# Sum into x, second norm and the next stage's first eight units in halves of 320 tokens, in a two-layer transformer trunk

## The chip, the cores and the metric

The kernel runs on one core of a Trainium2 chip. TensorE multiplies matrices, VectorE (DVE in the profile), ScalarE (ACT) and GpSimd (POOL) do elementwise work, SyncE (SP) issues most transfers; all follow their own instruction streams and meet at semaphores. The metric is the device time of one launch in microseconds (us). A change under about half a per cent can't be told from none.

## The reference

A trunk of two layers over two token streams, 512 sampled tokens and 128 prompt tokens, with model width 1024, all in float32. Each layer is:

```python
def trunk_layer(x, mod, g_mix_pre, g_mix_post, g_ffn_pre, g_ffn_post, w_ffn_in, w_ffn_conv, w_ffn_out, mixer):
    shift1, scale1, gate1, shift2, scale2, gate2 = mod
    h = rmsnorm(x, g_mix_pre) * (1 + scale1) + shift1
    y, ctx_state = mixer(h)
    x = x + gate1 * rmsnorm(y, g_mix_post)
    h = rmsnorm(x, g_ffn_pre) * (1 + scale2) + shift2
    x = x + gate2 * rmsnorm(conv_ffn(h, w_ffn_in, w_ffn_conv, w_ffn_out), g_ffn_post)
    return x, ctx_state
```

`rmsnorm` divides a token by the root of the mean of its squares over the 1024 features. `mixer` is a projection (12 blocks of 128 outputs in layer 0, 18 in layer 1), attention of several kinds and an output projection. `conv_ffn` projects to 2 x 2816, convolves each feature along the tokens with three taps, multiplies silu(gate) by value, and projects back. `mod` are six vectors per stream and layer, made from a conditioning vector by a wide projection.

## The kernel before

Everything is feature-major: a tensor is `[128 partitions, 8 blocks, 640 tokens]`, with the 512 sampled tokens ahead of the 128 prompt tokens. `x`, `y`, and the two parts `hh` and `hl` of the stage's input lie in SBUF.

A **unit** is one block of 128 outputs over all 640 tokens. A float32 product is made from three products of shorter numbers: weights `raw` (512 KB, loaded by SyncE) are split by ScalarE into a high part `whi` (`hi`, L499) and by VectorE into the rest `wlo` (`lo`, L793); the input is split the same way. `unit` (L1373, L1374) makes eight blocks x three products x two halves of 320 tokens, 48 matmuls; the first half's result goes to `bankA[s]`, the second's to `bankB[s]`, with s the parity of the unit. `raw`, `whi`, `wlo` and the banks all have two slots: the split for unit u+2 is made when unit u has been multiplied (`s_unit`), and SyncE loads weights n when the low part n-2 is made (`wide`, `s_lo`). The phases and their unit numbers stand in `UNITS`, and every wait counts in them.

Behind each unit the engines take its result out: in a feed-forward input phase (`fin0`, `fin1`, 22 units each, in pairs of gate and value) ScalarE copies the first half (L527), VectorE the second (L845), ScalarE makes the middle tap (L725), VectorE the two outer ones (L1143, L1146), and each pair ends with silu, gate product and a split into `ffh` and `ffl`. In layer 0 VectorE also sums a "modulation chunk" a pair (L801, two passes), a piece of the projection that makes `mod`, from a ring that SyncE loads (`chunk_in`), and SyncE waits for `s_mused` before it loads the next. In layer 1's input phase (`in`) VectorE applies the rotary embedding to four blocks (`rope`, L972 to L978) instead.

**The boundaries.** Three times a stage that makes `y` is followed by a sum into x, a second norm and a dense stage: post norm 1 then pre norm 2 (layer 0), post norm 3 then the pre norm 4 (into layer 1), post norm 5 then pre norm 6 (layer 1). There, before the change:

- `post_norm`: `deviation` (square root of the token sums, ScalarE), `reciprocal` (VectorE, L861), `spread` (TensorE copies the 640 inverse values to all partitions, L1438); then for each of the eight blocks VectorE multiplies y by the inverse rows (L867), adds gate times that to x (L899, once for each stream), ScalarE squares the new x (L534) and TensorE sums the squares over the features (`stat`, L1428).
- `pre_norm`: deviation, reciprocal and spread again; then for each block VectorE multiplies x by the inverse (L867), ScalarE scales and shifts (L557, once for each stream), and copies to `hh` (L563), and VectorE makes `hl` (L887).
- `first_pair` (L1486, L1487): the first two units of the next stage side by side, block by block as `hl` comes. All further units follow in order (`dense_pairs`).

## Time and profile before

| | us |
|---|---|
| median of 3 runs | 1804.48 |
| lowest, highest | 1798.44, 1805.21 |
| the profiled execution, its own time | 1804.35 |
| its span | 1802.6 |
| TensorE busy | 1659.5 (92%) |
| VectorE busy | 1092.2 (61%) |
| ScalarE busy | 722.5 (40%) |
| GpSimd busy | 114.5 (6%) |
| mean granted TensorE clock | 0.961 |

The span runs from the first to the last instruction of the profiled execution, and 1.8 us lie around it. Matmuls overlap, so a TensorE matmul's duration (0.31) is longer than the distance to the next one. Instructions of VectorE and ScalarE overlap the next by some 0.08.

### The profile page before, as it was taken

The page shows a single profiled execution, that of the slowest core. Times are in us where ns is not written, and L with a number is a line of the kernel's source. Part 1 is how long each engine was busy: PE and PEld are TensorE (multiplying, and loading weights), DVE is VectorE, ACT ScalarE, POOL GpSimd, SP SyncE. Part 2 cuts the span into 40 slices and gives each one's busy share as a digit, 9 for nine tenths or more (in the row PEclk, how much of TensorE's full clock was granted, in tenths as well). Part 3 has the DMA queues.
Part 4 walks back from the last instruction along what each step waited for, and adds up shares of the span by engine and source line. Part 5 has one row for each costly group of instructions (what it writes and reads, how often), then busy time and mean ns, then how long its engine had stood idle before and what let it go on. Part 6 is the DMA issues. An engine that isn't in the chain of part 4 may idle for free.

```text
span 1802.6 us, 33042 instructions
## 1 busy us (share of the span) xinstructions
PE 1659.5 (92%) x12288; PEld 1586.0 (88%) x12288; DVE 1092.2 (61%) x2046; ACT 722.5 (40%) x1186; POOL 114.5 (6%) x121
## 2 busy tenths in 40 slices
PE   5799899969999999999889979989799999999995
PEld 1799687959999999999889968779699999999995
DVE  4497676767777767777753248762566651466524
ACT  3722665226343134442241138652366541343410
POOL 1060210000000000000000032500000000000000
PEclk7899899979999999999999979999899999999998
DMA  8233001422434533345322110102012222222211
GB/s 295 89 110 124 31 2 48 157 77 72 118 113 142 199 116 114 105 145 193 120 79 81 48 62 2 45 1 62 32 59 71 80 81 72 70 71 80 92 49 59
DMA packets 42768, 160.63 MB, mean 89 GB/s; under 512 B 5072, under 2 KB 6096, under 8 KB 42304
## 3 DMA queue, kind: packets, MB, share of 16 engines
q1 hardware_dynamic: 39888, 152.00, 25.7%
q0 software_dynamic: 1584, 6.61, 1.1%
q8 instruction: 54, 0.88, 0.2%
q10 hardware_dynamic: 1216, 0.92, 0.2%
q14 instruction: 26, 0.21, 0.0%
HBM read 155.98 MB, written 3.54 MB: 88 GB/s over the span
## 4 chain that ended last, share of the span: by engine, by line
PE 79%; DVE 6%; issue 4%; ACT 2%; DMA 1%; DVEq 1%; ACTq 0%; SPq 0%
PE ps L1373 28%; PE ps L1374 28%; PE ps L1537 4%; PE ps L1566 4%; PE ps L1412 3%; PE ps L1552 3%; PE ps L1428 2%; PE ps L1486 1%; DMA ring<-in_wmodt 1%; DVE x L899 1%; PE ps L1487 1%; PE ps L1387 1%; PE ps L1386 1%; DVE ring L801 1%; DVE wlo L793 1%
## 5 line engine op out<-in xcount | busy, mean ns | idle before, releaser
L499 ACT ACTIVATE whi<-raw 128x1024 fp32r<-128x1024 f32 (+1 forms) x166 | 185.6, 1120 | 603.5 <-PE ps L1374 505.1
L1373 PE MATMUL ps<-hh,whi 128*128 128x320 f32 x920 | 286.7, 312 | 12.9 <-DVE wlo L793 12.9
L1373 PE MATMUL ps<-hl,whi 128*128 128x320 f32 x920 | 285.1, 310 | 0.0
L1373 PE MATMUL ps<-hh,wlo 128*128 128x320 f32 x920 | 285.1, 310 | 0.0
L1374 PE MATMUL ps<-hl,whi 128*128 128x320 f32 x920 | 285.0, 310 | 0.0
L1374 PE MATMUL ps<-hh,whi 128*128 128x320 f32 x920 | 284.9, 310 | 0.0
L1374 PE MATMUL ps<-hh,wlo 128*128 128x320 f32 x920 | 284.9, 310 | 0.0
L793 DVE TENSOR_TENSOR wlo<-raw,whi 128x1024 fp32r<-128x1024 f32 (+1 forms) x166 | 219.5, 1324 | 75.2 <-ACT whi L499 74.8
L1373 PEld LDWEIGHTS ps<-hh,whi 128*128 128x128 f32 x920 | 173.1, 188 | 14.5 <-DVE wlo L793 14.5
L1374 PEld LDWEIGHTS ps<-hh,whi 128*128 128x128 f32 x920 | 173.2, 188 | 0.0
L1374 PEld LDWEIGHTS ps<-hl,whi 128*128 128x128 f32 x920 | 173.2, 188 | 0.0
L1374 PEld LDWEIGHTS ps<-hh,wlo 128*128 128x128 f32 x920 | 173.2, 188 | 0.0
L1373 PEld LDWEIGHTS ps<-hh,wlo 128*128 128x128 f32 x920 | 173.1, 188 | 0.0
L1373 PEld LDWEIGHTS ps<-hl,whi 128*128 128x128 f32 x920 | 173.1, 188 | 0.0
L1428 PE MATMUL ps<-onesd,work 128*128 128x128 f32 x640 | 91.3, 301 | 31.3 <-ACT work L534 31.3
L1428 PEld LDWEIGHTS ps<-onesd,work 128*128 128x128 f32 x640 | 85.5, 212 | 36.1 <-ACT work L534 20.3
L653 ACT ACTIVATE pb<-pb,stat 128x640 f32<-128x640 f32 (+3 forms) x140 | 97.2, 697 | 11.6 <-DVE stat L1038 11.3
L1373 PE MATMUL ps<-ffh,whi 128*128 128x320 f32 x308 | 96.3, 313 | 0.0
L725 ACT ACTIVATE work<-work,wconv 128x642 f32<-128x642 f32 x88 | 73.5, 835 | 55.3 <-DVE work L845 36.1
L1373 PE MATMUL ps<-ffh,wlo 128*128 128x320 f32 x308 | 95.3, 310 | 0.0
L1373 PE MATMUL ps<-ffl,whi 128*128 128x320 f32 x308 | 95.3, 309 | 0.0
L1374 PE MATMUL ps<-ffh,wlo 128*128 128x320 f32 x308 | 95.3, 309 | 0.0
(209 smaller groups left out, 3322.1 us busy)
## 6 DMA issues: line engine op xcount, KB each, us to landing
raw<-in_w SPq DMA_DIRECT2D x134, 512.0 KB, 3.6
work<-in_wmodt SPq DMA_DIRECT2D x54, 512.0 KB, 3.6
raw<-in_w SPq DMA_DIRECT2D x32, 704.0 KB, 4.2
ring<-in_wmodt SPq DMA_DIRECT2D x26, 512.0 KB, 3.7
work<-in_wmod SPq DMA_DIRECT2D x16, 512.0 KB, 5.0
work<-in_rpb POOLq DMA_DIRECT2D x8, 480.0 KB, 4.3
x<-in_x SPq DMA_DIRECT2D x1, 2560.0 KB, 17.4
out_x<-x SPq DMA_DIRECT2D x8, 320.0 KB, 2.2
```

The lines of the kernel that those rows point to most:

```text
L499: nc.scalar.activation(whi[:, s, 0:kk * P], raw[:, s, 0:kk * P], ACT.Copy).then_inc(s_hi, 1)
L653: nc.scalar.activation(probs, probs, ACT.Exp, bias=negm, scale=-1.0, accum_out=sums[:, job.unit, half:half + 1]).then_inc(s_p, 1)
L725: nc.scalar.activation(cb[s], ub[s][:, 1:1 + CW], ACT.Copy, scale=wconv[:, bass.ds(2 * h + (2 * f0 + s), 1), 1]).then_inc(s_c1, 1)
L793: V.tensor_tensor(wlo[:, s, 0:kk * P], raw[:, s, 0:kk * P], whi[:, s, 0:kk * P].bitcast(F32), ALU.subtract).then_inc(s_lo, 1)
L801: last = V.scalar_tensor_tensor(out=out, in0=ring[b], scalar=1.0, in1=cwide[:, st, :], op0=ALU.mult, op1=ALU.mult, accum_out=mod[:, st, ba ...
L1373: T.matmul(bankA[s], slot(w, s, k), h[:, k, 0:HT], start=st, stop=sp_)
L1374: last = T.matmul(bankB[s], slot(w, s, k), h[:, k, HT:NT], start=st, stop=sp_)
L1412: last = T.matmul(out, h[:, k, t * P:(t + 1) * P], w[:, :, k * P:(k + 1) * P], start=k == 0 and n == 0, stop=k == KD - 1 and n == 2)
L1428: ins = T.matmul(token_sums[:, t, :], sq[s][:, t * P:(t + 1) * P], onesd[:, :], start=first and t in (0, 4), stop=last and t in (3, 4))
L1537: ins = T.matmul(scores_of(job, c, c + w), q[job.rows, job.pair, job.q0:job.q0 + P], k[job.rows, job.kslot, k0:k0 + w], start=n == 0, stop ...
L1552: T.transpose(turned_probs[half][:, c:c + P], pb[j % 4][:, c:c + P], ident[:, :])
L1566: T.matmul(values_bank[job.rows, 0:P], v[:, t, job.v_col:job.v_col + DH], pts[:, job.half, c:c + P], start=i == 0, stop=i == len(keys) - 1)
```

## The change

At the three boundaries the tokens are treated in halves of 320. The first half (tokens 0 to 319) is all sampled tokens; the second has 192 sampled and 128 prompt tokens. A class `Half` holds each half's token range and its semaphores. The next stage's first eight units are made twice: first all eight for the first half (`half_unit` on `bankA`, 24 matmuls each), then all eight for the second (`bankB`). As only two units' weights fit, SyncE loads these eight a second time and ScalarE and VectorE split them a second time, so every unit number behind a boundary rises by eight (`OFF`, `evicted`). The first half's results are parked in `y` (or `qk` for layer 1's input) as they come. The convolution, the gate and the rotary embedding need both halves and follow the second pass, where ScalarE takes the first half from `y` and not from the bank. Sums of squares, deviation, reciprocal and spread exist once for each half. The order on each engine is written out by hand in three functions called `norm_boundary`. In layer 0 SyncE's queue around the first modulation chunks is written anew. The work of the two norms on each element is the same.

The diff, cut to its core:

```diff
-            for n in (22, 23, 24):
+            for n in range(22, 28):
                 wide(n, n % 2, w8, n, 8)
-            sp.wait_ge(s_t, 24)
+            sp.wait_ge(s_mused, 26)
             chunk_in(26, 1, ring1)
-            wide(25, 1, w8, 25, 8)
+            for j in range(4):
+                wide(28 + j, j % 2, w8, 20 + j, 8)
             sp.wait_ge(s_mused, 27)
             chunk_in(27, 1, ring1)
+            for j in range(4, 6):
+                wide(28 + j, j % 2, w8, 20 + j, 8)
...
+            def half_squares(m, half, k0, k1):
+                for k in range(k0, k1):
+                    act.wait_ge(half.stat, half.squares(m) + k + 1)
+                    act.wait_ge(half.tu, half.items(m - 1) + k + 3)
+                    act.nop(nofuse=True)
+                    nc.scalar.activation(sq[k % 2][:, half.f:half.t], x[:, k, half.f:half.t],
+                                         ACT.Square).then_inc(half.sq, 1)
...
+            def half_high(m, half, layer, which, k0, k1):
+                part_ = 0 if which == 0 else 3
+                for k in range(k0, k1):
+                    s = k % 2
+                    act.wait_ge(half.t_, half.items(m) + k + 1)
+                    act.wait_ge(half.hl, half.made(m) + k + 1)
+                    for st, f, e in half.segments:
+                        last = nc.scalar.activation(hf[s][:, f:e], tn[s][:, f:e], ACT.Identity,
+                                                    scale=coef[:, layer, st, which, k:k + 1],
+                                                    bias=mod_col(layer, part_, st)[:, k:k + 1])
+                    last.then_inc(half.tu, 1)
+                    act.wait_ge(half.tu, half.items(m) + k + 3)
+                    nc.scalar.activation(hh[:, k, half.f:half.t], hf[s][:, half.f:half.t],
+                                         ACT.Copy).then_inc(half.hh, 1)
...
+            def norm_boundary(n, phase, ready, evac):
...
+                def split_and_take(j):
+                    act.wait_ge(s_unit, ua + j + 3)
+                    hi(j % 2, KD, (ua + j) // 2 + 1)
+                    evac(j, j % 2)
...
+                deviation(n)
+                half_squares(m, FIRST, 0, 8)
+                half_deviation(m, FIRST)
+                act.wait_ge(s_coef, ready)
+                half_high(m, FIRST, layer, which, 0, 8)
+                half_squares(m, SECOND, 0, 2)
+                split_and_take(0)
+                split_and_take(1)
+                half_squares(m, SECOND, 2, 4)
+                split_and_take(2)
+                split_and_take(3)
+                half_squares(m, SECOND, 4, 8)
+                split_and_take(4)
+                half_deviation(m, SECOND)
+                split_and_take(5)
+                half_high(m, SECOND, layer, which, 0, 3)
+                split_and_take(6)
+                half_high(m, SECOND, layer, which, 3, 6)
+                split_and_take(7)
+                half_high(m, SECOND, layer, which, 6, 8)
...
-                    copy_a(ub[s][:, 1:1 + HT], s)
-                    act.wait_ge(s_fa, u + 3)
-                    act.wait_ge(s_fb, u + 3)
+                    if parked:
+                        nc.scalar.activation(ub[s][:, 1:1 + HT], part(y, 2 * h + s, 0, HT), ACT.Copy).then_inc(s_park, 1)
+                        act.wait_ge(s_park, 2 * h + (8 * layer + s + 1))
+                    else:
+                        copy_a(ub[s][:, 1:1 + HT], s)
+                        act.wait_ge(s_fa, u + (3 - OFF[phase]))
+                    act.wait_ge(s_fb, u + (3 - OFF[phase]))
...
+            def norm_boundary(n, phase):
...
+                def split_for(j):
+                    dve.wait_ge(s_unit, ua + j + 3)
+                    lo(j % 2, KD, ua + j + 2)
+
+                reciprocal(n)
+                dve.wait_ge(s_row, n + 1)
+                post_items(FIRST, 0, 8)
+                post_items(SECOND, 0, 4)
+                half_reciprocal(m, FIRST)
+                dve.wait_ge(s_row, m + 1)
+                pre_row(FIRST, 0)
+                pre_row(FIRST, 1)
+                for k in range(KD):
+                    half_low(m, FIRST, k)
+                    pre_row(FIRST, k + 2)
+                post_items(SECOND, 4, 6)
+                split_for(0)
+                split_for(1)
+                post_items(SECOND, 6, 8)
+                split_for(2)
+                split_for(3)
+                split_for(4)
+                half_reciprocal(m, SECOND)
+                split_for(5)
+                dve.wait_ge(SECOND.row, SECOND.index(m) + 1)
+                pre_row(SECOND, 0)
+                pre_row(SECOND, 1)
+                for k in range(KD):
+                    if k == 2:
+                        split_for(6)
+                    if k == 5:
+                        split_for(7)
+                    half_low(m, SECOND, k)
+                    pre_row(SECOND, k + 2)
...
+            def half_unit(half, u, off, chunks=None):
+                bank, free = ((bankA, s_fa), (bankB, s_fb))[half.second]
+                cols = slice(half.f, half.t)
+                both = (u, u + 1) if chunks is not None else (u,)
+                pe.wait_ge(s_lo, both[-1] + 1)
+                pe.wait_ge(free, both[-1] + 1 - off)
                 for k in range(KD):
+                    if chunks is not None:
+                        pe.wait_ge(half.hl, chunks + k + 3)
+                    for v in both:
+                        for n, (w, h) in enumerate(((whi, hh), (whi, hl), (wlo, hh))):
+                            ins = T.matmul(bank[v % 2], slot(w, v % 2, k), h[:, k, cols], start=k == 0 and n == 0,
+                                           stop=k == KD - 1 and n == 2)
+                        if k == KD - 1:
+                            ins.then_inc(s_unit, 1)
...
+            def norm_boundary(n, phase):
+                m = n + 1
+                ub_ = UNITS[phase][0]
+                ua = ub_ - 8
+                for k in range(KD):
+                    half_stat(m, FIRST, k)
+                half_spread(m, FIRST)
+                half_unit(FIRST, ua, evicted[0], FIRST.made(m))
+                half_unit(FIRST, ua + 2, evicted[0])
+                for k in range(2):
+                    half_stat(m, SECOND, k)
+                half_unit(FIRST, ua + 3, evicted[0])
+                for k in range(2, 5):
+                    half_stat(m, SECOND, k)
+                half_unit(FIRST, ua + 4, evicted[0])
+                for k in range(5, 8):
+                    half_stat(m, SECOND, k)
+                half_unit(FIRST, ua + 5, evicted[0])
+                half_spread(m, SECOND)
+                half_unit(FIRST, ua + 6, evicted[0])
+                half_unit(FIRST, ua + 7, evicted[0])
+                evicted[0] = OFF[phase]
+                half_unit(SECOND, ub_, evicted[0], SECOND.made(m))
+                for j in range(2, 8):
+                    half_unit(SECOND, ub_ + j, evicted[0])
...
-                        first_pair(u0, 8 * (2 * layer + 1))
-                        dense_pairs(u0 + 2, FH - 1)
+                        norm_boundary(norm_index(layer, 1), (layer, "fin0"))
+                        dense_pairs(u0 + 8, FH - 4)
```

## Rows read from the trace of the kernel before

**Rows 1.** The page: busy time, and the chain that ended last

```profile
PE 1659.5 (92%) x12288; PEld 1586.0 (88%) x12288; DVE 1092.2 (61%) x2046; ACT 722.5 (40%) x1186; POOL 114.5 (6%) x121
...
PE 79%; DVE 6%; issue 4%; ACT 2%; DMA 1%; DVEq 1%; ACTq 0%; SPq 0%
```

**Rows 2.** Timeline of ScalarE, layer 0's feed-forward input: start, duration, instruction

```profile
453.62 1.06 ACT L499 ACTIVATE whi<-raw 128x1024 fp32r<-128x1024 f32 x1 [2.77 <-PE ps L1374]
...
467.70 1.06 ACT L499 ACTIVATE whi<-raw 128x1024 fp32r<-128x1024 f32 x1 [2.77 <-PE ps L1374]
```

**Rows 3.** Timeline of VectorE at the three boundaries, first rows and a reciprocal

```profile
382.89 1.55 DVE L867 TENSOR_TENSOR work<-y,ps 128x640 f32<-128x640 f32 x2 [2.60 <-PE ps L1438]
...
887.83 1.55 DVE L867 TENSOR_TENSOR work<-y,ps 128x640 f32<-128x640 f32 x2 [1.47 <-PE ps L1438]
...
1279.57 1.55 DVE L867 TENSOR_TENSOR work<-y,ps 128x640 f32<-128x640 f32 x2 [1.47 <-PE ps L1438]
...
1297.27 0.19 DVE L861 RECIPROCAL std<-std 128x5 f32<-128x5 f32 x1 [2.85 <-ACT std L540]
```

**Rows 4.** Timeline of TensorE at the third boundary

```profile
1303.22 0.61 PE L1486 MATMUL ps<-hh,whi 128*128 128x320 f32 x1 [4.32 <-DVE hl L887]
...
1303.63 0.47 PE L1487 MATMUL ps<-hh,whi 128*128 128x320 f32 x1
...
1303.89 0.47 PE L1486 MATMUL ps<-hl,whi 128*128 128x320 f32 x1
...
1322.42 0.41 PE L1373 MATMUL ps<-hh,whi 128*128 128x320 f32 x1 [2.98 <-DVE wlo L793]
```

**Rows 5.** Timeline of VectorE and SyncE behind the first boundary

```profile
423.80 1.23 DVE L793 TENSOR_TENSOR wlo<-raw,whi 128x1024 fp32r<-128x1024 f32 x1
...
436.12 0.33 SPq L396 DMA_DIRECT2D work<-in_wmodt  x1
...
436.48 1.21 DVE L793 TENSOR_TENSOR wlo<-raw,whi 128x1024 fp32r<-128x1024 f32 x1
```

**Rows 6.** Timeline of VectorE behind the second boundary

```profile
928.18 1.22 DVE L793 TENSOR_TENSOR wlo<-raw,whi 128x1024 fp32r<-128x1024 f32 x1 [0.65 <-ACT whi L499]
...
935.43 0.69 DVE L978 TENSOR_TENSOR qk<-y 128x512 f32<-128x512 f32 x1
```

**Rows 7.** Groups by shape: count | busy us, mean ns | idle before

```profile
L867 DVE TENSOR_TENSOR work<-y,ps 128x640 f32<-128x640 f32 x32 | 25.9, 821 | 10.9 <-PE ps L1438 7.0 <-DVE x L899 3.9
...
L899 DVE SCALAR_TENSOR_TENSOR x<-work,coef,x 128x512 f32 x24 | 17.9, 746 | 0.0
...
L899 DVE SCALAR_TENSOR_TENSOR x<-work,coef,x 128x128 f32 x24 | 8.3, 346 | 0.0
...
L845 DVE COPY y<-ps 128x320 f32 x26 | 12.7, 488 | 87.8 <-PE ps L1374 68.8 <-PE ps L1487 16.6 <-PE ps L1387 2.4
...
L557 ACT ACTIVATE work<-work,mod,coef 128x512 f32<-128x512 f32 x32 | 25.9, 810 | 11.2 <-DVE work L867 11.1
...
L557 ACT ACTIVATE work<-work,mod,coef 128x128 f32<-128x128 f32 x32 | 15.3, 480 | 0.0
...
L527 ACT ACTIVATE work<-ps 128x320 f32<-128x320 f32 x90 | 37.8, 420 | 0.0
```

**Rows 8.** The chain that ended last, one block of sums of squares

```profile
1257.54 1.11 PE ps L1428 x10
```

**Rows 9.** Timeline of VectorE behind the third boundary

```profile
1321.14 1.22 DVE L793 TENSOR_TENSOR wlo<-raw,whi 128x1024 fp32r<-128x1024 f32 x1 [1.90 <-ACT whi L499]
...
1332.89 1.23 DVE L793 TENSOR_TENSOR wlo<-raw,whi 128x1024 fp32r<-128x1024 f32 x1 [0.95 <-ACT whi L499]
```

**Rows 10.** The page, transfers: KB each, us from issue to landing

```profile
raw<-in_w SPq DMA_DIRECT2D x134, 512.0 KB, 3.6
```

**Rows 11.** Windows: stretch, us, busy by engine, granted TensorE clock, DMA

```profile
1302.90:1308.40 5.50, 5.18 (x22) 5.21 (x23) 4.11 (x7) 5.07 (x9) 0.00 (x0) 0.59 0.00 0
...
1322.40:1328.00 5.60, 5.58 (x38) 5.58 (x39) 4.64 (x7) 4.08 (x6) 0.00 (x0) 1.00 0.39 102
```

More of the change, by code:

```diff
@@ L1171, in ffn @@
             def ffn(layer):
[L1172 removed]
+                dve.wait_ge(SECOND.hl, SECOND.made(4 * layer + 2) + 8 + 2)
                 for s in range(2):
@@ new lines, in half_spread @@
+            def half_spread(m, half):
+                pe.wait_ge(half.rec, half.index(m) + 1)
+                if half.second:
+                    pe.wait_ge(s_t, FIRST.items(m))
+                    pe.wait_ge(half.t_, half.items(m))
+                c0 = 8 if half.second else 0
+                rows = half_rows[half.second]
+                for i, (c, r) in enumerate(((0, 0), (P, 0), (2 * P, 64))):
+                    w = P - r
+                    ins = T.matmul(rows[:, c:c + w], std[:, c0 + i:c0 + i + 1].to_broadcast([P, P]), ident[:, r:P],
+                                   start=True, stop=True)
+                ins.then_inc(half.row, 1)
```

203 lines of the change are left out of this document (142 added, 61 removed).

## The prediction

> **What bounds the kernel now.** I read the page's first part and its chain of waits first: TensorE is busy 92% of the span, and 79% of the chain that ended last is TensorE's [rows 1]. So wherever the dense units run, the time is TensorE's. One unit (48 matmuls of 320 columns) takes 7.04 us: in the stretch at 454 us the split of every second unit starts 14.08 us after the last, twice 7.04 [rows 2]. Time can be won only where TensorE stands still, and time is lost wherever it is made to.
>
> The change touches three boundaries, which I call A (layer 0, attention output to feed-forward), B (layer 0 to layer 1) and C (layer 1, attention output to feed-forward). I count each from the first post-norm row on VectorE (time 0) to the first matmul of the ninth unit behind it. The timelines show for C: time 0 at 1279.57, the second norm's reciprocal 17.7 later, the first dense matmul 23.65 later, the third unit 42.85 later [rows 3, 4]. Six more units make 42.2, so the ninth unit starts at 85.1. In A and B the low split that releases the third unit starts 40.9 and 40.35 in [rows 3, 5, 6] and takes 1.23, so the third unit starts at 42.2 and 41.6, the ninth at 84.4 and 83.8. Eight units are 56.3 of each, so a boundary now costs some 28 us of idle TensorE. That is all that could be won: three times 28.
>
> **Durations used.** On VectorE 640 columns take 0.82 and 320 take 0.49; the next instruction starts 0.08 before that ends, so a row of 320 costs 0.41. The add to x is 0.75 for 512 columns and 0.35 for 128: about 0.55 for 320 in one piece, 0.42 and 0.35 for the second half's two pieces (192 and 128). On ScalarE a 320-column copy or square takes 0.42; the scale-and-shift 0.81 for 512 and 0.48 for 128, so 0.65 for 320 and 0.53 and 0.48 for two pieces [rows 7]. A weight split is 1.06 on ScalarE [rows 2] and then 1.23 on VectorE [rows 5]. A full block of sums of squares is ten matmuls in 1.11 [rows 8], so the half block's six are 0.68. A hand-over between engines or to an engine's own result is taken as 0.12 to 0.2. With these the old order gives 23.7 and 43.3 for C where the trace has 23.65 and 42.85, so I trust them to about half a microsecond.
>
> **The new order, step by step.**
> *First half to its first matmul.* Eight rows and adds of 320 columns pace at 0.41 + 0.47 + 0.2 = 1.08 and end at 8.4. Then VectorE does four items of the second half (1.2 each) before it looks at the deviation, which is ready at 10.5: the reciprocal goes at 12.8. Spread, row, scale, copy and low part (0.7, 0.49, 0.65, 0.42, 0.49 and five hand-overs) bring the first matmul at 16.7. Against 23.65 that wins 7.0.
> *First half's pair.* ScalarE's scale and copy pace each chunk at 1.2 where its six matmuls take 0.88, so the pair ends at 26.2; the split of the third unit's weights (1.06 + 1.23, begun when the first unit of the pair ends at 25.8) lets the third half-unit start at 28.4. Before, 42.85 stood here, but with 14.1 us of matmuls done against 7.0 now.
> *Six first-half units.* 6 x 3.52 = 21.1, and the second half's eight sum blocks and its spread now stand between them on TensorE: 9 x 0.68 = 6.1. Square 4 of the second half waits on ScalarE behind the split taken after the fourth half-unit and square 7 behind the fifth: 1.0 of waiting. They end at 56.6.
> *The split that comes late.* ScalarE makes three items of the second half (1.6 each), the split behind the seventh half-unit, three more items, and only then the split behind the eighth; VectorE's order is the same. The chain is: sixth half-unit ends at 48.8; split 1.1 and copy 0.4; row 0 waits for VectorE's low split, 51.6; three items to 56.6; split and copy to 58.1; three items to 62.9; split 1.1, low split 1.23: 65.5. TensorE, done at 56.6, waits 8.9, because its second-half pair wants both weights. All chunks but the last are ready by then: the pair runs at full pace, 7.0, ending at 72.5. Behind it the next split again: the third second-half unit starts at 75.0 (76.3 in C, where the loop head loads a function table on ScalarE as it did before).
> *Three pairs of second-half units.* Here the evacuation that used to lie under 14.08 us of matmuls lies under 7.04: per pair four taps on VectorE, two low splits, copies, gate. The trace of before shows this cycle when TensorE does not set it, in the first pair behind each boundary. In C low split to low split but one is 11.75 [rows 9]; in A, with a modulation chunk of two 1.22 passes in it, 12.7 [rows 5]; in B a pair with two ropes is 8.5 (low split at 928.18, last rope done at 936.1, next copies) [rows 6]. So C pays 3 x 11.75 = 35.3, B 8.5 + 8.5 + 7.0 = 24.0. In A the first of the three is longer: SyncE's queue now holds the weights of the fifth second-half unit behind a wait for the modulation chunk that VectorE makes last in the pair, 12.2 after its low split (the next chunk's issue stands at 436.12) [rows 5]; issue 0.5, landing 3.6 [rows 10] and split 1.1 make 17.6. A pays 17.6 + 12.7 + 12.7 = 43.0.
> *Queues.* 24 more weight loads of 512 KB land in 3.6; outside the case in A they are issued a unit ahead and hidden. POOL's loads for layer 1 wait for the second half's last low part instead of the whole's; nothing waits for them.
>
> **The clock.** In C the pause of 4.3 before the first dense matmul left the clock at 1.2 GHz for most of the next 5.5 us (0.59 granted); the pause of 3.0 before 1322.42 left it at full clock [rows 4, 11]. At 1.2 GHz the first matmuls start 0.265 apart [rows 4] against 0.147. I add 1.5 a boundary for twelve such matmuls behind the new pause of 8.9; the first pair has the same in both. The Trainium skill (TensorE: Matmul & The Clock Gate, HAM oscillation) says that a loop whose bursts are short against its waits falls to the low clock at every turn; by that rule the second-half pairs would run at 0.265 too. The rows agree for one pause and not for the other, so it is a rival below.
>
> **Sum.** Ninth unit: A 75.0 + 43.0 = 118.0 against 84.4, +33.6. B 75.0 + 24.0 = 99.0 against 83.8, +15.2. C 76.3 + 35.3 = 111.6 against 85.1, +26.5. With the clock 3 x 1.5: +79.8. Behind the ninth unit TensorE sets the pace as before and gives nothing back. The profiled execution took 1804.35, within 0.2 us of the median: 1884.
>
> **Bounds.** Hand-overs between 0.08 and 0.16 move the sum by 5 either way. The clock term is 0 to 9 in all (no pause slows anything, or each new pause of more than 2 costs 1.5 twice a boundary). The pair cycle of second-half units is at least VectorE's own busy work (about 10.0 in C, 11.0 in A, for the gaps could close when the copy of the first half comes from SBUF): -11 in all. SyncE's wait in A is 0 to 5.
>
> **Rivals.**
> *The evacuation keeps up (0.13).* If second-half pairs ran at TensorE's 7.04, each ninth unit would start at 75.0 + 21.1 = 96.1, 97.4 in C: +11.7, +12.3, +12.3, with the clock +41, 1845. Against it: the rows of 11.75 and 12.7 are durations of this same code.
> *The low clock in the second pass (0.12).* 48 matmuls at 0.265 are 12.7 a pair: nothing in A, +1 a pair in C, +4.2 a pair in B, and the second-half pair itself 4.3 more at each: +29, 1912.
> *Not slower (0.05).* One mechanism: VectorE and ScalarE, once the third half-unit runs, always have the next split ready. Then a boundary costs 28.4 + 21.1 + 6.1 + 7.0 + 21.1 = 83.7 against 84.4: 1.4 won at most in C, 1802 in all. It decides from a late split under 1 us and a pair cycle under 7.04; the rows of before put the cycle 1.5 to 5.7 above.
> *Forecast (0.70).* 1866 to 1900 by its own bounds.
>
> **Range and chances.** 1856 to 1906 takes in the forecast's own bounds and the lower part of the clock case, and leaves out the keeping-up case, the rest of the clock case and the not-slower one. No change can be told from a change under 0.5% (9 us) here. Faster needs more than the whole of the fourth case: 0.02; same 0.03; slower 0.95.
>
> **What would show it.** Right: the first dense matmul of each boundary 16 to 18 us behind the first post-norm row; some 8 to 10 us of TensorE idle before the second-half pair, put down to the low split; pauses of 4 to 10 us between pairs of second-half units in A and C, 1.5 in B; a pause near 10 in A with the load of raw behind a wait on SyncE. TensorE's busy time stays near 1660. Wrong: second-half pairs at 7 us, or a late split under 3 us; then a VectorE instruction of 320 columns or the order on ScalarE was misread.

## The result and the profile after

| | before | changed |
|---|---|---|
| median | 1803.28 (1798.44 to 1805.21, 4 runs) | 1888.28 (1881.5 to 1888.54, 4 runs) |
| ratio | | 1.0467, 95% interval 1.0435 to 1.0498 |
| a second series of runs, beside the experiments | 1800.91 | 1882.84, ratio 1.0439 (1.0410 to 1.0467) |
| span of the profiled execution | 1802.6 | 1886.5 |

Slower by 82 to 85 us: 1884 was predicted, with a range of 1856 to 1906. The page of the changed kernel, its busy times and the start of its chain, to be held against [rows 1]:

```profile
PE 1690.3 (90%) x12342; PEld 1611.0 (85%) x12342; DVE 1130.2 (60%) x2169; ACT 750.5 (40%) x1289; POOL 114.6 (6%) x121
...
PE 75%; DVE 9%; ACT 3%; issue 3%; DMA 2%; DVEq 0%; ACTq 0%; SPq 0%
```

TensorE has 54 matmuls more (sums and spreads in halves) and 31 us more of busy time, a good part of it because more matmuls run at the low clock. The view of waits on TensorE (us in all, times, longest) shows where it stands still. L1894 is the matmul of `half_unit`, L912 the low split of weights; before, the low split cost it 12.9 us in `unit`, and `half_unit` did not exist.

```profile
PE ps L1894 <- DVE wlo L912: 60.5, 16, 11.2
...
PE ps L1578 <- DVE wlo L912: 13.4, 4, 3.9
```

The timeline places these waits. Only the rows of VectorE's first post-norm row (time 0) and those of TensorE after a pause stand here; the bracket is the pause and what ended it. Boundary A:

```profile
384.26 0.89 DVE L1027 TENSOR_TENSOR work<-y,ps 128x320 f32<-128x320 f32 x2 [2.59 <-PE ps L1645]
...
399.74 0.60 PE L1894 MATMUL ps<-hh,whi 128*128 128x320 f32 x1 [2.44 <-DVE hl L1043]
...
410.95 0.41 PE L1894 MATMUL ps<-hh,whi 128*128 128x320 f32 x1 [2.12 <-DVE wlo L912]
...
446.92 0.64 PE L1894 MATMUL ps<-hh,whi 128*128 128x320 f32 x1 [7.50 <-DVE wlo L912]
...
458.44 0.64 PE L1894 MATMUL ps<-hh,whi 128*128 128x320 f32 x1 [2.14 <-DVE wlo L912]
...
478.42 0.63 PE L1894 MATMUL ps<-hh,whi 128*128 128x320 f32 x1 [11.18 <-DVE wlo L912]
...
491.14 0.41 PE L1894 MATMUL ps<-hh,whi 128*128 128x320 f32 x1 [3.69 <-DVE wlo L912]
...
503.74 0.61 PE L1578 MATMUL ps<-hh,whi 128*128 128x320 f32 x1 [3.76 <-DVE wlo L912]
```

The first dense matmul is at 15.5, the third half-unit at 26.7, the second-half pair at 62.7, the third second-half unit at 74.2, the next pairs at 94.2 and 106.9, and the ninth unit (first of L1578) at 119.5. The same for C, timeline of the changed kernel:

```profile
1335.18 0.89 DVE L1027 TENSOR_TENSOR work<-y,ps 128x320 f32<-128x320 f32 x2 [1.47 <-PE ps L1645]
...
1399.96 0.64 PE L1894 MATMUL ps<-hh,whi 128*128 128x320 f32 x1 [7.52 <-DVE wlo L912]
...
1412.44 0.41 PE L1894 MATMUL ps<-hh,whi 128*128 128x320 f32 x1 [3.42 <-DVE wlo L912]
...
1423.96 0.41 PE L1894 MATMUL ps<-hh,whi 128*128 128x320 f32 x1 [3.73 <-DVE wlo L912]
...
1435.46 0.42 PE L1894 MATMUL ps<-hh,whi 128*128 128x320 f32 x1 [2.68 <-DVE wlo L912]
...
1447.15 0.38 PE L1578 MATMUL ps<-hh,whi 128*128 128x320 f32 x1 [3.92 <-DVE wlo L912]
```

C reaches the second-half pair at 64.8, and then 77.3, 88.8, 100.3 and 112.0, where [rows 3, 4] and six more units give 85.1. In B, read in the same way, the ninth unit starts at 99.2 (83.8 before). So the ninth units come 35.1, 15.4 and 26.9 us later: 77.4 together. The spans agree. From time 0 of A to that of B it is 542.95 against 504.94 before, from B to C 407.97 against 391.74, from C to the end 551.3 against 523.0, in all 82.5 more. The 5 us on top of 77.4 lie mostly behind the ninth unit: the first units there still run at the low clock. In windows of 33 us from there on in C (36 in A) the changed kernel does 215 matmuls (227), where the one before does 225 (245), at 0.147 each 1.5 us in C and 2.6 in A. The window view of the one before, then of the changed kernel (columns: stretch, its length, TensorE's busy time and matmuls, granted clock, DMA share, GB/s):

```profile
425.08:461.08 36.00, 36.00 (x245) 1.00 0.42 132
...
1322.42:1355.42 33.00, 33.00 (x225) 1.00 0.28 86
```

```profile
503.74:539.74 36.00, 36.00 (x227) 0.92 0.39 126
...
1447.15:1480.15 33.00, 32.99 (x215) 0.95 0.26 80
```

### The profile page after: what moved, and what is told of

Its sections match the earlier page's. It is cut to its first block, busy times and chain, and to the rows that moved or that the text cites. A ratio compares the mean times of both kernels' runs of the same rounds, so it can differ in the third digit from the quotient of the medians.

```text
span 1886.5 us, 33320 instructions
## 1 busy us (share of the span) xinstructions
PE 1690.3 (90%) x12342; PEld 1611.0 (85%) x12342; DVE 1130.2 (60%) x2169; ACT 750.5 (40%) x1289; POOL 114.6 (6%) x121
## 4 chain that ended last, share of the span: by engine, by line
PE 75%; DVE 9%; ACT 3%; issue 3%; DMA 2%; DVEq 0%; ACTq 0%; SPq 0%
PE ps L1579 24%; PE ps L1578 24%; PE ps L1894 6%; PE ps L1743 4%; PE ps L1772 3%; PE ps L1614 3%; PE ps L1758 3%; DVE wlo L912 2%; ACT whi L538 1%; DMA ring<-in_wmodt 1%; PE ps L1633 1%; DVE work L1027 1%; PE ps L1591 1%; PE ps L1590 1%; DVE x L1034 1%
## 5 line engine op out<-in xcount | busy, mean ns | idle before, releaser
L538 ACT ACTIVATE whi<-raw 128x1024 fp32r<-128x1024 f32 (+1 forms) x190 | 210.5, 1110 | 623.2 <-PE ps L1579 465.8
L912 DVE TENSOR_TENSOR wlo<-raw,whi 128x1024 fp32r<-128x1024 f32 (+1 forms) x190 | 249.0, 1312 | 126.8 <-ACT whi L538 126.3
L1578 PE MATMUL ps<-hh,whi 128*128 128x320 f32 x776 | 242.8, 313 | 13.4 <-DVE wlo L912 13.4
L1579 PE MATMUL ps<-hh,whi 128*128 128x320 f32 x776 | 241.4, 311 | 0.0
L1578 PE MATMUL ps<-hl,whi 128*128 128x320 f32 x776 | 241.4, 311 | 0.0
L1579 PE MATMUL ps<-hl,whi 128*128 128x320 f32 x776 | 241.2, 311 | 0.0
L1579 PE MATMUL ps<-hh,wlo 128*128 128x320 f32 x776 | 241.2, 311 | 0.0
L1578 PE MATMUL ps<-hh,wlo 128*128 128x320 f32 x776 | 241.1, 311 | 0.0
L1894 PE MATMUL ps<-hh,whi 128*128 128x320 f32 x384 | 131.6, 343 | 67.8 <-DVE wlo L912 60.5
L1578 PEld LDWEIGHTS ps<-hh,whi 128*128 128x128 f32 x776 | 146.8, 189 | 14.7 <-issue 8.2
L1579 PEld LDWEIGHTS ps<-hl,whi 128*128 128x128 f32 x776 | 147.0, 189 | 0.0
L1579 PEld LDWEIGHTS ps<-hh,whi 128*128 128x128 f32 x776 | 147.0, 189 | 0.0
L1578 PEld LDWEIGHTS ps<-hl,whi 128*128 128x128 f32 x776 | 146.8, 189 | 0.0
L1579 PEld LDWEIGHTS ps<-hh,wlo 128*128 128x128 f32 x776 | 146.8, 189 | 0.0
L1578 PEld LDWEIGHTS ps<-hh,wlo 128*128 128x128 f32 x776 | 146.7, 189 | 0.0
L1894 PEld LDWEIGHTS ps<-hh,whi 128*128 128x128 f32 x384 | 80.7, 210 | 72.4 <-DVE wlo L912 64.7
L1894 PE MATMUL ps<-hl,whi 128*128 128x320 f32 x384 | 127.7, 333 | 0.0
L1894 PE MATMUL ps<-hh,wlo 128*128 128x320 f32 x384 | 127.3, 331 | 0.0
L763 ACT ACTIVATE pb<-pb,stat 128x640 f32<-128x640 f32 (+3 forms) x140 | 97.2, 697 | 11.6 <-DVE stat L1240 11.3
L964 DVE COPY work<-ps 128x192 f32<-128x192 f32 (+1 forms) x180 | 49.7, 319 | 80.6 <-PE ps L1579 66.6
L1578 PE MATMUL ps<-ffh,whi 128*128 128x320 f32 x308 | 96.3, 313 | 0.0
## 6 DMA issues: line engine op xcount, KB each, us to landing
x<-in_x SPq DMA_DIRECT2D x1, 2560.0 KB, 17.6
```

The lines of the kernel that those rows point to most:

```text
L538: nc.scalar.activation(whi[:, s, 0:kk * P], raw[:, s, 0:kk * P], ACT.Copy).then_inc(s_hi, 1)
L763: nc.scalar.activation(probs, probs, ACT.Exp, bias=negm, scale=-1.0, accum_out=sums[:, job.unit, half:half + 1]).then_inc(s_p, 1)
L912: V.tensor_tensor(wlo[:, s, 0:kk * P], raw[:, s, 0:kk * P], whi[:, s, 0:kk * P].bitcast(F32), ALU.subtract).then_inc(s_lo, 1)
L964: last = V.tensor_copy(dst, bankB[s][:, f:f + n])
L1578: T.matmul(bankA[s], slot(w, s, k), h[:, k, 0:HT], start=st, stop=sp_)
L1579: last = T.matmul(bankB[s], slot(w, s, k), h[:, k, HT:NT], start=st, stop=sp_)
```

## The experiments

Ten runs. Timed ratios carry some 0.3% either way (5 us), and the stretch ahead of A, where the code is the same, took 375 to 384 us from one profile to the next. So the single effects are read from the timelines, behind time 0. A "cycle" is the time from the start of one pair of second-half units to the next, beginning with the third and fourth unit. This table gives the start of the ninth unit behind time 0, read as above; for the kernel before it is the third unit's start and 42.2 (its trace has the ninth units at 84.5, 84.0 and 85.2). Two kernels whose runs are told by themselves are not in it.

| kernel | A | B | C | sum | ratio to before (95% interval) |
|---|---|---|---|---|---|
| before | 84.4 | 83.8 | 85.1 | 253.3 | 1 |
| changed | 119.5 | 99.2 | 112.0 | 330.7 | 1.0467 (1.0435 to 1.0498) |
| changed, second profile | 120.7 | 100.7 | 111.9 | 333.3 | 1.0439 (1.0410 to 1.0467) |
| split sooner | 118.3 | 95.7 | 108.7 | 322.7 | 1.0400 (1.0375 to 1.0425) |
| loads first | 111.9 | 100.0 | 111.1 | 323.0 | 1.0409 (1.0382 to 1.0435) |
| short taps | 113.9 | 100.8 | 107.4 | 322.1 | 1.0358 (1.0317 to 1.0400) |
| no table loads | 117.9 | 100.8 | 106.1 | 324.7 | 1.0434 (1.0405 to 1.0462) |
| busy in the pause | 115.5 | 98.3 | 111.1 | 324.9 | 1.0406 (1.0376 to 1.0435) |
| two passes, full norm | 121.4 | 99.9 | 115.0 | 336.3 | 1.0459 (1.0427 to 1.0491) |
| three repairs | 106.3 | 95.7 | 105.0 | 307.0 | 1.0337 (1.0307 to 1.0366) |

**The changed kernel again.** No edit.

> The changed kernel as it is, run beside the next three, so that each can be compared with it on the same chip. It should stand 4.4 to 4.9% above the kernel before, near 1884.

1882.84 us. Its profile shows how far one execution differs from the next: the six first-half units, from the third half-unit to the second-half pair, take 36.0 us in A and B of the first profile and 37.5 in C, and 37.5 at all three boundaries of the second. The pause behind them is 7.5 every time. The difference is the clock: the window view of the first profile, A and then C.

```profile
410.95:439.40 28.45, 27.87 (x198) 1.00 0.41 130
1362.45:1392.45 30.00, 29.42 (x198) 0.94 0.31 106
```

The same 198 matmuls take 1.55 us longer at a granted 0.94, and which of the two it is changes from one execution to the next.

**Halved norms alone.** The first pair is made for each half in turn, and all else is as before the change.

```diff
-                half_unit(FIRST, ua, evicted[0], FIRST.made(m))
-                half_unit(FIRST, ua + 2, evicted[0])
...
+                half_pair(FIRST, FIRST.made(m))
+                for k in range(KD):
                     half_stat(m, SECOND, k)
...
                 half_spread(m, SECOND)
...
-                for j in range(2, 8):
-                    half_unit(SECOND, ub_ + j, evicted[0])
+                half_pair(SECOND, SECOND.made(m))
```

> Only the halved norms are kept: no unit is made twice. The first pair is made for the first half of the tokens, then for the second, and all further units are full. By the durations of the prediction the first matmul comes near 16, but the third unit must wait for the whole second half: eight items of the post norm and eight of the pre norm on ScalarE and VectorE at 1.2 and 1.6 us behind the first half's end, about 53 us behind the first post-norm row where 42.85 stood before. So the ninth unit starts some 9 to 10 us later at each boundary, 29 us in all, near 1830. If an earlier first matmul is worth what it wins, the kernel is 10 to 20 us faster than before. If the loss of the change lies mainly in the halved norms, this kernel is near 1870.

1827.15 us, ratio 1.0147 (1.0123 to 1.0171): 26 us slower than before, where 29 was expected. Its timeline in C:

```profile
1288.44 0.88 DVE L1008 TENSOR_TENSOR work<-y,ps 128x320 f32<-128x320 f32 x2 [1.47 <-PE ps L1615]
...
1303.81 0.60 PE L1876 MATMUL ps<-hh,whi 128*128 128x320 f32 x1 [2.43 <-DVE hl L1024]
...
1323.61 0.63 PE L1876 MATMUL ps<-hh,whi 128*128 128x320 f32 x1 [2.57 <-DVE hl L1024]
...
1337.46 0.63 PE L1548 MATMUL ps<-hh,whi 128*128 128x320 f32 x1 [3.42 <-DVE wlo L893]
```

The first dense matmul is at 15.4, 8.3 us sooner than before, and the third unit at 49.0, 6.2 us later than the 42.85 of [rows 4]; A and B have 49.1 and 47.9 against 42.2 and 41.6. The three delays are 19.3 of the 26 us. The rest is the low clock behind the third unit: 231, 216 and 203 matmuls where the kernel before does 245, 227 and 222 in windows as long, 6.5 us in all. By the trace its ninth units come 25.7 us later than those of the kernel before, the whole of the timed loss. An early first matmul is worth nothing if the second half comes later.

**Two passes alone.** Full-width norms in front, the two half passes behind.

```diff
                 for k in range(KD):
...
+                    stat(m, k, k % 2)
+                spread(m)
                 half_unit(FIRST, ua, evicted[0], FIRST.made(m))
...
+                for j in range(2, 8):
+                    half_unit(FIRST, ua + j, evicted[0])
...
-                half_unit(SECOND, ub_, evicted[0], SECOND.made(m))
+                half_unit(SECOND, ub_, evicted[0], 0)
```

> The two norms are again full width, as before the change; only the two passes over the first eight units, with their second load and second split, are kept. The first matmul is then at 23.7 us behind the first post-norm row and the third half-unit near 38; six half-units whose splits are 3.5 us apart end near 60, with no wait for a late split but some waits for the two splits of 2.3 us and the load of raw; the second-half pair and its three cycles are as in the changed kernel. By the prediction's steps (the loss lies in the second pass: 43, 24 and 35 us where 21 would do) this kernel is within 5 us of the changed one, 80 us slower than before. If the loss came from the halved norms instead (their many small instructions and the squeezed order), this kernel would stand near the old one, within 20 us of it.

1905.77 us, ratio 1.0586 (1.0550 to 1.0623), 21 to 26 us above the changed kernel by the ratios and not within 5. The expectation missed a wait that this experiment had kept: in the changed kernel `stat` waits until all eight rows of the norm ahead are multiplied (`s_t`), and with full-width norms this holds the first sum until all eight blocks are done. The timeline of this kernel in C shows it:

```profile
1360.44 10.78 PE L1589 MATMUL ps<-onesd,work 128*128 128x128 f32 x72 [13.14 <-DVE work L969]
```

Against a pause of 3.64 before the change. The first dense matmul came at 31.0 (31.2 in B) and not 23.65. So this run compares nothing cleanly, and was repeated without that wait.

**Two passes, full norm, without that wait.** The edit against the kernel just told:

```diff
                 if first and n:
                     pe.wait_ge(s_std, n)
-                if first and n > 1:
-                    pe.wait_ge(s_t, 8 * n)
                 pe.wait_ge(s_sq, k + (8 * n + 1))
```

> As the kernel with full-width norms and two passes, but without a wait that the changed kernel added ahead of the sums of squares and that held them until all eight blocks of the post norm were done (13 us of pause at each boundary). The first matmul should be back at 23.7 us behind the first post-norm row. From there that run took 96 us in A and 88.6 us in C to the ninth unit; so the ninth unit would start at 120 in A and 112 in C, where the changed kernel has 119.5 and 112.0. In all this kernel is within 6 us of the changed kernel: the second pass alone costs the whole loss. If the mended wait is not what made the other 21 us slower than the changed kernel, it stays there.

1884.10 us, ratio 1.0459 (1.0427 to 1.0491), between the two ratios of the changed kernel. The first dense matmul is at 23.7 again. Its timeline in A (time 0 at 380.04), first dense matmul and second-half pair:

```profile
403.73 0.60 PE L1846 MATMUL ps<-hh,whi 128*128 128x320 f32 x1 [4.32 <-DVE hl L989]
...
446.86 0.63 PE L1846 MATMUL ps<-hh,whi 128*128 128x320 f32 x1 [2.56 <-DVE wlo L895]
```

So the second pass alone gives the whole loss. The halved norms give next to nothing back on top of it: they start the first half 8 us sooner, but the second-half pair starts at 66.8, 66.7 and 67.6 here against 62.7 to 65.7 in the changed kernel, and the ninth units differ by 3 to 6 us in sum, too little for the timed ratios. 5 of the 8 us go in the longer pause ahead of that pair, 7.5 us against 2.56 here.

**Split sooner.** The split behind the eighth first-half unit, one of the two that the second-half pair waits for, comes two items earlier on ScalarE and one earlier on VectorE.

```diff
-                half_high(m, SECOND, layer, which, 3, 6)
+                half_high(m, SECOND, layer, which, 3, 4)
                 split_and_take(7)
-                half_high(m, SECOND, layer, which, 6, 8)
+                half_high(m, SECOND, layer, which, 4, 8)
...
-                    if k == 5:
+                    if k == 4:
                         split_for(7)
```

> One change: on ScalarE and VectorE the split behind the eighth first-half unit (the one that releases the second-half pair) stands behind four second-half items of the pre norm and not behind six (five on VectorE instead of six on the two engines' own count). If the wait of some 7.5 us before the second-half pair is the order of these two streams, as the prediction said, two items of 1.6 us come after the split and it shrinks to about 4 us at each of the three boundaries: 10 us less than the changed kernel in all, near 1878. If the wait is set by something else (the load of raw, the sixth unit's end), the time stays within 2 us of the changed kernel. If the items pushed behind the split then hold up the pair's last chunks, the pair takes longer than 9 us and the gain is below 6.

1873.07 us, ratio 1.0400. The pair in A:

```profile
442.42 0.41 PE L1894 MATMUL ps<-hh,whi 128*128 128x320 f32 x1 [4.39 <-DVE wlo L912]
```

The pause before the second-half pair falls from 7.5 to 4.39 at all three boundaries, so 1.56 for each of the two items that ScalarE no longer makes ahead of the split (the prediction priced one at 1.6). The sum of the ninth units falls by 8 to 11 us. In A it is only 1.2 us against the first profile of the changed kernel (where the first-half units had run 1.5 us faster) and 2.5 against the second: the next pause grows to 11.7, from 11.2 and 10.7, because there the next load is tied to something else.

**Loads first.** SyncE issues the weights of the fifth and sixth second-half units ahead of its wait for the modulation chunk (layer 0).

```diff
-            for j in range(4):
+            for j in range(6):
                 wide(28 + j, j % 2, w8, 20 + j, 8)
             sp.wait_ge(s_mused, 27)
             chunk_in(27, 1, ring1)
-            for j in range(4, 6):
-                wide(28 + j, j % 2, w8, 20 + j, 8)
```

> One change, in layer 0 alone: SyncE issues the weights of the fifth and sixth second-half units before it waits for the modulation chunk and loads the next one. If the pause of 11.2 us between the first two second-half pairs of boundary A is longer than the others because that load stands behind the wait, it falls to about 4 to 6 us and the kernel gains 5 to 7 us over the changed one, near 1882. If VectorE's evacuation sets this pause too, the time stays within 2 us. The modulation chunk comes one load later; it was used 12 us after and should not be late.

1873.22 us, ratio 1.0409. This is the something else. Timeline of the changed kernel in A, between the first two second-half pairs (SPq is SyncE's queue):

```profile
468.28 1.22 DVE L920 SCALAR_TENSOR_TENSOR work<-work,cwide 128x1024 f32<-128x1024 f32 x1
...
469.54 0.33 SPq L432 DMA_DIRECT2D work<-in_wmodt  x1
469.91 8.98 SPq L411 DMA_DIRECT2D raw<-in_w  x3
...
476.06 1.06 ACT L538 ACTIVATE whi<-raw 128x1024 fp32r<-128x1024 f32 x1 [9.82 <-DMA raw<-in_w]
...
477.14 1.23 DVE L912 TENSOR_TENSOR wlo<-raw,whi 128x1024 fp32r<-128x1024 f32 x1 [7.17 <-ACT whi L538]
```

VectorE ends the modulation chunk at 469.5, SyncE then issues the next chunk (469.54) and only then the weights (469.91), ScalarE has them at 476.06, after 9.82 of idle time, and VectorE after 7.17. In the kernel with the loads first the raw weights are issued at 454.37 and TensorE's pause is 3.96 instead of 11.18:

```profile
454.40 0.63 PE L1892 MATMUL ps<-hh,whi 128*128 128x320 f32 x1 [2.14 <-DVE wlo L910]
...
467.12 0.41 PE L1892 MATMUL ps<-hh,whi 128*128 128x320 f32 x1 [3.96 <-DVE wlo L910]
```

The cycle goes from 20.0 to 12.7, as long as the two behind it, and A's ninth unit comes 7.6 us sooner (8.9 against the second profile). Nothing at B and C.

**Short taps.** In `fin0` of both layers the two outer taps cover 64 columns; the rest of these taps is left out.

```diff
+                    tw = 64 if half == 0 else CW
-                    V.scalar_tensor_tensor(out=cb[s], in0=ub[s][:, 0:CW], ...
+                    V.scalar_tensor_tensor(out=cb[s][:, 0:tw], in0=ub[s][:, 0:tw], ...
```

> In the first half of the pairs of both feed-forward input phases the two outer taps of the convolution cover 64 columns and not all (the rest of those two taps is left out, so the output is another). This takes 4 x 0.6 = 2.4 us of VectorE's work from a pair and leaves every wait and hand-over as it is. If VectorE's work sets the 11.5 us cycle of the second-half pairs, six such cycles in A and C shrink by 1.2 to 2.4 each: 7 to 14 us less than the changed kernel. If ScalarE, SyncE's queue or the chain of hand-overs sets it, the cycle stays and the time is within 3 us of the changed kernel. The full-width pairs behind have TensorE as their bound and give nothing.

1862.74 us, ratio 1.0358; in the timeline the ninth units come 8.6 to 11 us sooner in sum. The rest of the 15 to 20 us lies elsewhere in the execution, mostly ahead of A, where the code is the same and this profile took 375.0 us against 384.3 and 380.5. The cycle of the second-half pairs falls in A from 12.7 and 12.6 to 10.4 and 10.3, all of the 2.4 us that were cut, and in C from 11.5 to 10.3, half of them. So VectorE's work sets the cycle in A, and something else helps to set it in C.

**No table loads.** Silu is replaced by a square, which leaves the function itself out.

```diff
-                        nc.scalar.activation(sg, cb[0], ACT.Silu).then_inc(s_sg, 1)
+                        nc.scalar.activation(sg, cb[0], ACT.Square).then_inc(s_sg, 1)
```

> ScalarE's silu in all feed-forward input phases is replaced by a square (the output is another), which needs no function table of its own: the two table loads of 1.28 us in each pair are gone. In the 11.5 us cycle of the second-half pairs no engine is busy all the time (VectorE about 9, ScalarE about 9). If the cycle is a chain that goes from ScalarE's high split to VectorE's taps, the gate, the ffh copy, a table load and the next high split, only the second of the two loads lies on it: each cycle shortens by 1.3 to 10.2 us, six cycles in A and C give 8 us less than the changed kernel, near 1875. If VectorE's work alone sets the cycle nothing changes; if ScalarE's does, each cycle loses 2.6 us and the gain is 15.

1877.95 us, ratio 1.0434: not to be told from the changed kernel by its time. The timeline tells more. Cycles in C fall from 11.5, 11.5 and 11.7 to 10.5, 10.2 and 10.3, and the one of the pair ahead of them from 12.5 to 10.9; in A they stay at 12.7 and 12.6. The expectation had the mechanism right and the place half wrong: the trace of the changed kernel has no table load in A's cycles, only one at 449.2, ahead of them. The chain in C, timeline of the changed kernel:

```profile
1428.92 0.89 DVE L1348 SCALAR_TENSOR_TENSOR work<-work,wconv 128x642 f32<-128x642 f32 x1
...
1430.02 0.69 DVE L1354 TENSOR_TENSOR work<-work 128x512 f32<-128x512 f32 x1 [0.21 <-DVE work L1348]
1430.63 0.28 DVE L1355 TENSOR_TENSOR work<-work 128x128 f32<-128x128 f32 x1
1431.04 0.74 ACT L848 ACTIVATE ffh<-work 128x640 f32 x1 [1.25 <-DVE work L1355]
1431.80 1.28 ACT L538 ACT_TABLE_LOAD   x1
...
1433.09 1.06 ACT L538 ACTIVATE whi<-raw 128x1024 fp32r<-128x1024 f32 x1
...
1434.18 1.23 DVE L912 TENSOR_TENSOR wlo<-raw,whi 128x1024 fp32r<-128x1024 f32 x1 [0.95 <-ACT whi L538]
```

and in the kernel with the square:

```profile
1410.28 0.74 ACT L848 ACTIVATE ffh<-work 128x640 f32 x1 [2.67 <-DVE work L1355]
1410.93 1.04 ACT L538 ACTIVATE whi<-raw 128x1024 fp32r<-128x1024 f32 x1
...
1412.39 1.22 DVE L912 TENSOR_TENSOR wlo<-raw,whi 128x1024 fp32r<-128x1024 f32 x1
```

From the last tap the chain goes over the gate on VectorE to the `ffh` copy on ScalarE, then one table load, then the next high split, then the low split that lets TensorE on. From `ffh` to the low split it is 3.14 us with the load and 2.11 without, where VectorE comes to it straight from its copies, with no wait. Of the two loads in a pair only the second lies on this chain. The Trainium skill (ScalarE: Activation LUTs, What ACT_TABLE_LOAD costs) puts 1.38 us of draining beside the 1.28 of the load itself; here the `ffh` copy ends at 1431.78 and the load starts at 1431.80, the split follows at 1433.09, so this trace shows only the 1.28.

**Busy in the pause.** 48 matmuls whose result nobody uses, between the eighth first-half unit and the second-half pair.

```diff
                 evicted[0] = OFF[phase]
+                for i in range(48):
+                    T.matmul(psf[:, 2704:2704 + HT], hh[:, 0, 0:P], hh[:, i % KD, 0:HT], start=True, stop=True)
                 half_unit(SECOND, ub_, evicted[0], SECOND.made(m))
```

> One change: 48 matmuls of 320 columns on data that is already there, with their result in an unused part of PSUM, stand on TensorE between the eighth first-half unit and the second-half pair. They fill 7.0 us of the 7.5 us wait. If the pair took 9.0 us and not 7.0 because the pause left TensorE at the low clock, it now starts at full clock, takes 7.0 and each boundary gains 1.5 to 2 us: 5 us less than the changed kernel in all. If the length of the pair is set by its last chunks (the second half's low parts) nothing is won; if the extra matmuls run at the low clock themselves, each boundary loses up to 5 us.

1872.84 us, ratio 1.0406. The pair in A, window view, of the changed kernel and then of this one:

```profile
446.90:456.00 9.10, 9.08 (x48) 0.74 0.18 58
```

```profile
442.60:449.70 7.10, 7.08 (x48) 1.00 0.23 76
```

The same 48 matmuls take 9.1 us at a granted 0.74, and 7.1 at full clock. From the start of the pair to the third second-half unit it is 9.4, 9.4 and 10.7 us in A, B and C instead of 11.5, 11.4 and 12.5 (11.3, 11.3 and 12.4 in the second profile). So the clock costs nearly 2 us a boundary there, 5.5 to 5.8 in all, and the pair had full clock where TensorE had not stopped. The timed gain, 6 us by the ratios against the neighbour run, is not clear of the intervals; the ninth units come 5.8 to 8.5 us sooner in sum. In A the next cycle is 2.0 us shorter as well (18.0 against 20.0; but the second profile of the changed kernel has 18.5 without any such matmuls).

**Three repairs together.** Split sooner, loads first, and 28 extra matmuls in what is left of the pause.

> Three repairs together: the earlier split, the weights of two more second-half units ahead of SyncE's wait, and 28 extra matmuls on TensorE in what is left of the pause before the second-half pair (4.1 us of 4.4). Alone the first two gave 7 to 12 and 6 to 10 us and 48 extra matmuls gave 6 to 10; the last and the first share the same pause. If each acts in its own place the kernel stands 20 to 23 us below the changed one, near 1861, and still some 60 us above the kernel before, because the cycles of the second-half pairs and what is left of the late wait stay. If the repairs act on the same time, it stays near 1870.

1859.38 us, ratio 1.0337 (1.0307 to 1.0366): 18 to 23 us below the changed kernel, as expected of places that don't overlap, and still 59 above the kernel before. Its ninth units start at 106.3, 95.7 and 105.0, 24 to 26 us sooner in sum; the profiled execution was the fastest of its four, 10 us below their median, with full clock in all the first-half units. What is left in A and C is 4 us of the late wait, filled with useless matmuls, and three cycles of 11.5 to 12.7 where TensorE has work for 7.04. None of the experiments points to an order that beats the kernel before: halved norms alone lose, the second pass alone loses.

## Why the prediction was right

**The total.** +79.8 was predicted; the two series gave +85.0 and +81.9. The mechanism held step by step, but that the total came so near is partly luck, because errors of both signs met. By the first profile, over the three boundaries: the second-half pair started 6.3 us sooner in sum than predicted, the way from there to the third second-half unit was 5.6 longer, the three cycles 2.8 longer. That makes 77.4 for the ninth units where the sum had 75.3, and the 4.5 added for the clock met about 5 behind the ninth units, for which the sum had no term.

**The first half.** First dense matmul at 16.7: it came at 15.4 to 15.7, in the second profile up to 16.0. VectorE's rows with their adds came every 0.98 (rows of L1027 at 385.64 and 386.62) where 1.08 was taken, and the reciprocal stood at 11.8 and not 12.8. Third half-unit at 28.4: 26.7, 26.7 and 27.3, and up to 28.1 in the second profile, where the pair ran longer at the low clock. The later one matters: it moved the whole first pass.

**The late split.** A wait of 8.9 was predicted, 7.5 was measured, at each boundary of both profiles. The mechanism (items of the second half ahead of the split, on ScalarE) stands by the run with the split sooner: 1.56 us an item. The pair was predicted at 65.5 and came at 62.7, 62.7 and 64.8, in the second profile at 65.7, 65.6 and 64.7.

**The second-half pair.** 7.0 at full pace plus a clock term of 1.5: it took 9.1, so the clock cost 2.0 and not 1.5. "All chunks but the last are ready" held: with TensorE kept busy the pair took 7.1.

**The second pass.** This is the step that carried the forecast, and it held: C 11.5, 11.5 and 11.7 against 11.75; A 12.7 and 12.6 against 12.7; B 8.6, 9.4 and 7.1 in the first profile and 8.3, 8.3 and 7.1 in the second, against 8.5, 8.5 and 7.0. Taking the cycle from the first pair behind each boundary of the kernel before was enough.
The size that was off is A's first cycle, 17.6 predicted (its four terms as written add up to 17.4) and 20.0 measured in one profile, 18.5 in the other. The cause was named rightly (weights behind the wait for the chunk) and shown by the run with the loads first. What was short is the way from issue to split: SyncE issued the raw at 469.91 and ScalarE began at 476.06, 6.15 us, and 4.62 in the second profile, where the prediction had 3.6 of landing [rows 10] and 0.5 of issue. The chain view of the changed kernel gives it to the load:

```profile
469.91 6.04 DMA raw<-in_w
```

SyncE issues three transfers of 512 KB there within a microsecond (the chunk at 469.54, raw at 469.91 and 470.39). With the loads first the same raw, issued at 454.37 with no other beside it, landed after 3.8. That fits transfers that share their time; why two profiles of one kernel differ by 1.5 us in it stays open.

**The clock** was sized too small. In the first profile it cost 5.8 in the three second-half pairs, 2.6 in A and 1.5 in C behind the ninth unit, 1.5 in C's first-half units and 1.3 in B's cycles: 12.7. In the second profile it is 5.5, 1.5 and 1.5 (235 and 215 matmuls in the windows of 36 and 33 us) and 1.5 at each of the three boundaries: 13. The sum took 4.5 and its own bound ended at 9, so this term lay outside its bound.

**The signs.** Those of being wrong (second-half pairs at 7 us, a late split under 3) did not come. Those of being right came near but mostly not within their numbers: the first dense matmul at 15.4 to 16.0 for 16 to 18, the late wait 7.5 for 8 to 10, the pauses between pairs in A and C 2.6 to 3.9 for 4 to 10 (the cycles were as forecast, but the pairs took 7.8 to 9.0 of them and not 7.0). The pause in A behind the wait on SyncE was 11.2 and 10.7 for "near 10".

**TensorE's busy time** was predicted near 1660 and is 1690. The low clock is part of this: a matmul there counts 0.47 or more of busy time and not 0.31, also in A's second-half pairs, where it cost no time. How the 31 us divide was not worked out.

**The rivals.** *The evacuation keeps up*: refuted by the cycles and by the run with short taps, where less work on VectorE made them shorter. *The low clock in the second pass* is half there: A's pairs and some of C's run at the low clock in part, but a wait on the evacuation covers it. In B it shows once: behind a pause of 2.1 the first cycle ran at a granted 0.81, and the first two took 8.6 and 9.4 us; in the second profile, at 1.00, they took 8.3 each. The rule of the Trainium skill (TensorE: Matmul & The Clock Gate, HAM oscillation), that a loop whose bursts are short against its waits falls to the low clock at every turn, agrees with the second-half pairs behind the 7.5 us pause (0.74 to 0.78 granted) and with A (0.79 to 0.84 from 456.0 to 503.7); in C the pairs behind pauses of 3.42 and 2.68 had 1.00, those behind 3.73 had 0.85. *Not slower*: it needed a late split under 1 us and a cycle under 7.04, and neither came near.

The two experiments that undo one half of the change each say more than the forecast did: the halved norms alone cost 26 us, the second pass alone 83, and both together cost 82 to 85 and not 109. The likely reason, which no run separates: under the first pass's half-units the work of the halved norms is hidden, and without them it lies bare.

## What to carry to other kernels

Before work is cut in halves to fill a pause, look for what was hidden behind the whole: here the evacuation of a pair lay under 14 us of matmuls, and under half the tokens it had 7, while the weight splits didn't shrink at all. Such a cycle can be read off the kernel as it is, from the place where TensorE has just restarted. Where a hand-written order puts a release (a split, a load) behind other work on an in-order engine or queue, count the items ahead of it: here each was worth its own length (1.56 us) in the consumer's pause, and moving two of them behind the split did not lengthen the pair.

## What the runs showed of the hardware

- The clock doesn't come back with the work. After a pause of 7.5 us 48 matmuls took 9.1 us instead of 7.1, after one of 3.8 to 3.9 the following 33 to 36 us of uninterrupted matmuls held 4 to 7% fewer of them (4% after 2.57 in the second profile's A). With useless matmuls in the pause the granted clock stayed at 1.00.
- The same kernel takes the same stretch at a granted 1.00 or 0.94, from one execution to the next and from one boundary to the next, with the pauses of 2.43, 2.12 and 7.5 us around it equal to 0.02 us: 36.0 or 37.5 us. The pause before the half's spread did differ, but not in step: 2.12 and 2.33 where it was 36.0, 2.05 to 2.60 where it was 37.5. So a pause's length alone did not tell the clock behind it.
- A function-table load on ScalarE shows as 1.28 us and no more, and where it isn't on the chain of hand-overs it costs nothing: of two in each pair one counted. In layer 0 the same loop has none, and in layer 1 the changed kernel has them in four pairs and none in the pairs behind; why was not asked.
- Useless matmuls made TensorE busier (1700.1 us of busy time against 1690.3) while the kernel's median was 10 us below that of its neighbour run (1872.84 against 1882.84) and its ninth units came 5.8 to 8.5 us sooner: a busy share says little about time.
